# A mixture-of-experts layer on one core: when the weight splits of a step are made, how many buffers hold them, and in which order the last step does its work

## The chip, the cores and the metric

The kernel runs on one core of a Trainium2 chip. Times are device microseconds of one execution. The engines are TensorE (PE, with its weight loads as PEld), VectorE (DVE), ScalarE (ACT), GpSimd (POOL) and SyncE (SP, which here only issues DMAs). Each engine works through its own list of instructions in order and waits on semaphores.

## The reference

One layer (pooling mixer), then a mixture-of-experts MLP, then a final norm. The weights of the experts are 32 x (1024 x 1024 gate/up and 512 x 1024 down) float32, 201 MB in all, and are read once.

```
h = rms_norm(x, norm_mix); x = x + pool_mixer(h, pool_w, pool_scale)
h = rms_norm(x, norm_ffn)                       # 1024 tokens x 1024
g_sel = argmax(h @ w_rg + b_rg)                 # one of 4 groups
top 2 of the 8 experts of that group, gates = p_group * softmax share
for each expert e, its tokens:
    g, up = split(xt @ w_gu[e]); y = (silu(g) * up) @ w_down[e]
    x[tokens] += gate * y
return rms_norm(x, norm_final)
```

## The kernel before, in words

**Tiling.** The 32 experts are 32 steps; each gets one block of 128 rows (64 rows in the "small" steps 5, 7, ..., 27, which are handed the experts with few tokens). The rows are gathered from DRAM by POOL (`xg`), turned by PE (`turn_x`), and split into a high part (`x_hi`, ACT) and a low rest (`x_lo`, DVE), since fp32 products are made of three products of fp32r parts (hi x hi, hi x lo, lo x hi). The weights come as *pairs*: 1 MB each, 128 x 2048 float32, six to a step: four gate/up pairs and two down pairs, 192 in all, numbered in the order of use. `start(s) = 6 s - 2` is the number of the first gate/up pair of step s; pairs start(s)+4 and start(s)+5 are the down pairs of step s-1, used in step s.

**A pair's way.** SP loads it into a raw slot (L504; at most four loads in flight, L546; and a raw slot must be free, L540). ACT copies it to a high buffer (`split_pair`, L884). DVE subtracts (`low_pair`, L1210), and the low part takes the raw slot's place. PE uses both (12 matmuls for a full pair, L1724; 8 in a small step's gate/up pair, L1736) and frees both.

**Buffers.** There are 18 raw slots and 3 high buffers. `GIVEN` turns raw slots over to high buffers: two at step 4 (16 and 5) and two more at step 22 (14 and 7). Which slots are the last to be used, `end_raw`, follows from that; in the end five of them take the tiles of the output (`end_tile`) and the last step's h.

**A step on ACT** (`step` in the ACT program, from step 4 on). With n = `lead(s)`: split pairs up to start(s)+n; then, if step s-1 was small, `copy_lower`, `split_x_block(s)`, one more pair, `silu_of_sums(s-1)`; otherwise `silu_block(s-1)` and `split_x_block(s)`; pairs up to start(s)+n+2; `split_h_block(s-1)`; `copy_y` of step s-2, which POOL then scatters and adds to `total` in DRAM. `silu_block(s-1)` waits until PE has used the four gate/up pairs of step s-1. `lead` is 2, and 3 in step 29, 4 from step 30.

**A step on DVE** mirrors it with n = lead(s)-1: low parts up to start(s)+n; `add_lower`, `low_x`, one more low part and `hidden_of_sums` after a small step, otherwise `hidden` and `low_x`; low parts up to start(s)+n+3; `low_h`.

**A step on PE**: four gate/up pairs of s (with `turn_x(s+1)` ahead of the last), down pair, `turn_h(s)`, down pair. After a small step, `turn_h(s-1)` comes behind the first gate/up pair of s. Step 32 has only the two down pairs of step 31.

**The end.** When the scatter of step 28 has landed (`y_stored`), SP loads the eight tiles of `total` (L562) and POOL gathers the rows of the last three steps, whose y never goes through DRAM (L772). ACT makes eight sums of squares and roots (`final_square`, L816, L822) and three for the late rows (`late_squares`); DVE makes eight norms (`final_norm`, L1547, L1548), adds the last three y (`late_add_copied`, `late_add`) and makes three late norms. SP stores the eight tiles (L565); when all have landed, POOL scatters the late rows over them, one after the other (L777). ACT loads a table each time it goes between silu and square root.

Of the kernel before, what the change touches and what calls it, by code (L numbers as in the profile page):

```python
# [28 lines left out]
def hybrid_pool_moe(nc, x, norm_mix, norm_ffn, norm_final, pool_w, pool_scale,  # L29
# [3 lines left out]
    ALU, ACT, AX = mybir.AluOpType, mybir.ActivationFunctionType, mybir.AxisListType.X  # L33
# [3 lines left out]
    TILES = TOKENS // P  # L37
# [4 lines left out]
    E = w_re.shape[2]  # L42
# [9 lines left out]
    PER_STEP = (KD + KF) // 2  # L52
# [6 lines left out]
    HEAD = 4  # L59
    RANKED = E - HEAD - 3  # L60
    LATE, IN_BANKS = 3, 2
    FREE_STEP = HEAD
    GIVEN = {HEAD: 2, E - 10: 2}
    SPARE = sum(GIVEN.values())

    gu_rows = w_gu[0].rearrange("e (p k) f -> e p (k f)", k=KD)
# [8 lines left out]
    with ctx:  # L75
        def sem(name):
            return ctx.enter_context(nc.semaphore(name))
# [9 lines left out]
        def small(name, shape, dt):  # L87
            return ctx.enter_context(nc.sbuf_tensor(name, shape, dt))
# [34 lines left out]
        for m in range(MAIN):  # L123
            for _ in range(next((n for s, n in GIVEN.items() if m == s * PER_STEP - (PER_STEP - GU_PAIRS)), 0)):
                in_hi.append(in_raw.pop())
# [9 lines left out]
        end_free = [in_raw[r] + 1 for r in end_raw]  # L135
# [124 lines left out]
        eps = small("eps", [P, 1], f32)  # L260
# [4 lines left out]
        warm = small("warm", [P, 2], f32)  # L265
# [93 lines left out]
        pair_used = sem("pair_used")  # L359
# [15 lines left out]
        nfin_in = sem("nfin_in")  # L375
# [44 lines left out]
        def start(s):  # L420

            return s * PER_STEP - (PER_STEP - GU_PAIRS)

        def lead(s):

            return min(4, 2 + max(0, s - (E - LATE - 1)))

        def pw_low(eng, h):

# [29 lines left out]
        def place(m):  # L459

            s, j = next((s, j) for s in range(FREE_STEP, E + 1) for j in parts(s) if pair(s, j) == m)
            return s, s, j

        def up_to(following, one, s, n):

            while following[0] < min(start(s) + n, MAIN):
                one(*place(following[0]))
                following[0] += 1
# [341 lines left out]
        def _(act):  # L810
# [177 lines left out]
            def early_step(s):  # L988

                for j in parts(s):  # L990
                    if s == 0 and j == 0 or s == 1 and j < GU_PAIRS:
                        continue
                    if s > 1 and j == 0:
                        silu_block(s - 1, pair(s - 1, GU_PAIRS - 1) + 1)
                        split_x_block(s)
                    if s == 0 and j == 2:
                        router_exps()
                        act.wait_ge(slotted, 1)
                    if s == 0 and j == 3:
                        split_first_x()  # L1000
                    if s >= 1 and j == h_split_at(s):
                        split_h_block(s - 1, None if s == 1 else pair(s - 1, PER_STEP - 1) + 1)
                    split_pair(s, s, j)
                    if s >= 2 and j == h_split_at(s):
                        gates_of_y(s - 2)
                        copy_y(gate_now[:] if s == 2 else gate_all[:, s - 2:s - 1], start(s), None if s == 2 else s - 2)
                    if s == 0 and j == GU_PAIRS - 1:
                        split_x_block(1)
                        for m in range(2):
                            split_pair(1, 1, m)  # L1010
                        silu_block(0, GU_PAIRS, Y)
                        for m in (2, 3):
                            split_pair(1, 1, m)

            def step(s, s0, turn):
                if s < FREE_STEP:
                    early_step(s)
                    return
                n = lead(s)
                up_to(split_next, split_pair, s, n)  # L1020
                if s == E:

                    act.wait_ge(pair_used, end_free[TILES // 2])
                    for i in range(3):
                        final_square(i, 0)
                    nc.scalar.activation(warm[:, 1:2], eps[:], ACT.Silu)
                if is_small(s - 1):

                    copy_lower(s - 1, start(s - 1) + GU_PAIRS)
                    split_x_block(s)  # L1030
                    up_to(split_next, split_pair, s, n + 1)
                    silu_of_sums(s - 1, small_turn(s - 1, 0))
                else:
                    silu_block(s - 1, start(s - 1) + GU_PAIRS)
                    if s < E:
                        split_x_block(s, is_small(s))
                up_to(split_next, split_pair, s, n + 2)
                if s == E:
                    final_square(3, 0)
                    split_h_block(s - 1, end_free[TILES // 2], hi=h2_hi)  # L1040
                else:
                    split_h_block(s - 1, start(s))
                if s < E - 1:
                    copy_y(gate_all[:, s - 2:s - 1], start(s), s - 2)
                if s == E - 1:

                    up_to(split_next, split_pair, s, 2 * PER_STEP)
                    act.wait_ge(pair_used, start(s))
                    act.wait_ge(y_stored, 16 * (E - LATE))
                    col = E - LATE  # L1050
                    nc.scalar.activation(ysb[:], Y, ACT.Identity, scale=gate_all[:, col:col + 1])\
                        .then_inc(y_copied, 1)

            def final_square(i, turn):

                act.wait_ge(y_in[i], 16 * (turn + 1))
                root_mean_square(end_junk[:], end_tile(i), i, ss, rs).then_inc(squares3, 1)

            split_next = [FIRST]
# [5 lines left out]
            def late_squares(k):  # L1065

                act.wait_ge(late_sum, k + 1)
                root_mean_square(end_junk[:], late_tile(k), k, ss2, rs2).then_inc(late_square, 1)

            for i in range(4, TILES):  # L1070
                final_square(i, 0)
            for k in range(LATE):
                late_squares(k)

            with act.If(n):

# [29 lines left out]
        def _(dve):  # L1106
# [409 lines left out]
            def step(s, s0, turn):  # L1516
                if s < FREE_STEP:
                    early_step(s)
                    return
                n = lead(s) - 1  # L1520
                up_to(low_next, low_pair, s, n)
                if s == E:
                    up_to(low_next, low_pair, s, PER_STEP)
                    dve.wait_ge(nfin_in, 16)
                    for i in range(3):
                        final_norm(i, 0)
                if is_small(s - 1):
                    add_lower(small_turn(s - 1, 0))
                    low_x(s)
                    up_to(low_next, low_pair, s, n + 1)  # L1530
                    hidden_of_sums(s - 1)
                else:
                    hidden(s - 1)
                    if s < E:
                        low_x(s, is_small(s))
                up_to(low_next, low_pair, s, n + 3)
                if s == E:
                    late_add_copied()
                    final_norm(3, 0)
                    low_h(s - 1, hi=h2_hi, lo=h2_lo)  # L1540
                else:
                    low_h(s - 1)

            def final_norm(i, turn):

                dve.wait_ge(squares3, turn * TILES + i + 1)
                link(V.reciprocal(rs[:, i:i + 1], rs[:, i:i + 1]))  # L1547
                V.scalar_tensor_tensor(end_tile(i), end_tile(i), rs[:, i:i + 1], nfin[:],  # L1548
                                       ALU.mult, ALU.mult).then_inc(out_made, 1)

            def late_add_copied():

                dve.wait_ge(late_in[0], 16)
                dve.wait_ge(y_copied, E - IN_BANKS)
                V.tensor_tensor(late_tile(0), ysb[:], late_tile(0), ALU.add).then_inc(late_sum, 1)

            def late_add(k, y, dn_end):

                col = E - LATE + k
                dve.wait_ge(late_in[k], 16)  # L1560
                dve.wait_ge(pair_used, dn_end)
                V.scalar_tensor_tensor(late_tile(k), y, gate_all[:, col:col + 1], late_tile(k),
                                       ALU.mult, ALU.add).then_inc(late_sum, 1)

            low_next = [FIRST]
# [10 lines left out]
                V.scalar_tensor_tensor(late_tile(k), late_tile(k), rs2[:, k:k + 1], nfin[:],  # L1576
                                       ALU.mult, ALU.mult).then_inc(late_made, 1)

            for i in range(4, TILES):
                final_norm(i, 0)  # L1580
            late_add(1, Y, MAIN - GU_PAIRS // 2)
            late_add(2, GU, MAIN)
            for k in range(LATE):
                late_norm(k)
# [308 lines left out]
```

## Time and profile before

| | |
|---|---|
| time, median of 3 runs | 662.93 us (660.96 to 665.18) |
| profiled execution | 663.27 us, of which the span is 661.5 us |
| PE, DVE, ACT busy | 94%, 92%, 81% of the span |
| mean granted clock of TensorE | 0.983 |
| DMA traffic | 242.83 MB, mean 367 GB/s |

The span runs from the first to the last instruction; the rest of the execution's time lies around it. A busy share is an average over stages with different limits, so it tells less than the waits of each stage.

### The profile page before, as it was taken

What the parts mean: (1) busy time and instruction counts of PE and PEld (TensorE: products, weight loads), DVE (VectorE), ACT (ScalarE), POOL (GpSimd) and SP (SyncE); (2) the same over time, 40 slices, a digit from 0 to 9 for tenths busy, and PEclk for the clock granted to TensorE, in tenths of its full rate; (3) what the DMA queues carried; (4) which work ended last, traced back from release to release, by engine and by line L of the source; (5) the groups of instructions that cost most, each with busy time, mean ns of one, the idle gap of its engine ahead of it and who ended that gap; (6) DMA issues with size and microseconds to landing.
All of it is one profiled execution on the core that took longest, in us unless ns stands there. A gap on an engine that the chain in (4) does not pass through costs nothing.

```text
span 661.5 us, 9555 instructions
## 1 busy us (share of the span) xinstructions
PE 622.6 (94%) x3460; PEld 526.4 (80%) x3460; DVE 606.2 (92%) x501; ACT 535.7 (81%) x458; POOL 157.9 (24%) x127
## 2 busy tenths in 40 slices
PE   6899989999999999999999999897999989989983
PEld 4799978887888888888888888686877868767872
DVE  5887688989999999999999999897989889998987
ACT  5996626688898989898988988887879688978794
POOL 5000010032222222222222222252225222340311
PEclk9999989999999999999999999999999989989997
DMA  8997769999999999999999999999999999999985
GB/s 293 421 418 278 244 209 374 397 343 302 322 381 404 390 400 393 386 401 374 402 367 401 364 401 366 402 379 392 381 384 386 385 413 384 410 409 400 380 335 211
DMA packets 43637, 242.83 MB, mean 367 GB/s; under 512 B 8184, under 2 KB 9344, under 8 KB 19011
## 3 DMA queue, kind: packets, MB, share of 16 engines
q1 hardware_dynamic: 34322, 220.39, 84.2%
q0 software_dynamic: 9264, 21.79, 12.1%
q8 instruction: 29, 0.48, 0.3%
q14 instruction: 22, 0.17, 0.1%
HBM read 227.19 MB, written 26.21 MB: 383 GB/s over the span
## 4 chain that ended last, share of the span: by engine, by line
DMA 54%; PE 34%; DVE 5%; ACT 3%; issue 2%; SPq 0%; POOL 0%; ACTq 0%; POOLq 0%; DVEq 0%
DMA raw<-in_expert_w_gu 32%; PE psum L1724 19%; DMA raw<-in_expert_w_down 17%; PE psum L1736 3%; PE psum L1652 3%; PE psum L1670 2%; DMA total<-ysb,src_all 2%; PE psum L1638 2%; DMA raw<-total 1%; PE psum L1776 1%; DMA pw_in<-in_pool_w 1%; PE psum L1661 1%; DVE raw L1548 1%; PE psum L1678 1%; PE psum L1787 1%
## 5 line engine op out<-in xcount | busy, mean ns | idle before, releaser
L1210 DVE TENSOR_TENSOR w_lo<-raw,w_hi 128x2048 fp32r<-128x2048 f32 x113 | 255.4, 2284 | 7.8 <-ACT w_hi L884 7.4
L884 ACT ACTIVATE w_hi<-raw 128x2048 fp32r<-128x2048 f32 x113 | 213.5, 1914 | 21.8 <-DMA raw<-in_expert_w_gu 12.8
L1210 DVE TENSOR_TENSOR w_lo<-raw,w_lo 128x2048 fp32r<-128x2048 f32 x79 | 178.5, 2283 | 2.4 <-ACT w_lo L884 2.3
L884 ACT ACTIVATE w_lo<-raw 128x2048 fp32r<-128x2048 f32 x79 | 149.5, 1914 | 13.2 <-DMA raw<-in_expert_w_gu 10.2
L710 POOL DMA_INDIRECT total<-ysb,src_all x28 | 53.5, 1910 | 338.5 <-ACT ysb L979 323.9
L1724 PE MATMUL psum<-w_lo,x_hi 128*128 128x512 f32 x432 | 127.1, 397 | 5.8 <-DVE x_lo L1446 5.8
L1724 PE MATMUL psum<-w_lo,h_hi 128*128 128x512 f32 x376 | 108.3, 395 | 0.5 <-DVE h_lo L1480 0.5
L1724 PEld LDWEIGHTS psum<-w_lo,x_hi 128*128 128x128 f32 x432 | 81.0, 190 | 23.2 <-DVE x_lo L1446 6.7
L696 POOL DMA_INDIRECT xg<-normed,src_all x31 | 78.2, 2523 | 21.5 <-DVE src_all L1305 12.3
L1724 PEld LDWEIGHTS psum<-w_lo,h_hi 128*128 128x128 f32 x376 | 70.9, 190 | 15.5 <-DVE h_lo L1480 0.9
L1736 PE MATMUL psum<-w_lo,x_hi 128*128 128x512 f32 x276 | 74.0, 392 | 0.0
L1724 PE MATMUL psum<-w_hi,x_hi 128*128 128x512 f32 x208 | 67.2, 405 | 5.1 <-DVE x_lo L1446 5.1
L1724 PE MATMUL psum<-w_hi,x_lo 128*128 128x512 f32 x208 | 64.8, 393 | 0.0
L1736 PEld LDWEIGHTS psum<-w_lo,x_hi 128*128 128x128 f32 x276 | 51.5, 188 | 10.6
L1724 PEld LDWEIGHTS psum<-w_hi,x_hi 128*128 128x128 f32 x208 | 37.8, 191 | 13.6 <-DVE x_lo L1446 6.4
L970 ACT ACTIVATE h_hi<-psum 128x512 fp32r<-128x512 f32 x32 | 19.1, 597 | 34.9 <-PE psum L1787 20.0
L1724 PEld LDWEIGHTS psum<-w_hi,x_lo 128*128 128x128 f32 x208 | 39.3, 189 | 8.5
L1724 PE MATMUL psum<-w_hi,h_hi 128*128 128x512 f32 x136 | 42.9, 397 | 0.0
L1724 PE MATMUL psum<-w_hi,h_lo 128*128 128x512 f32 x136 | 42.0, 390 | 0.0
L1724 PE MATMUL psum<-w_lo,h_lo 128*128 128x512 f32 x120 | 37.5, 394 | 0.0
L1724 PE MATMUL psum<-w_lo,x_lo 128*128 128x512 f32 x112 | 35.5, 399 | 0.0
L1776 PEld LDWEIGHTS psum<-ident,xg 128*128 128x128 f32 x256 | 33.4, 191 | 2.5
(208 smaller groups left out, 865.4 us busy)
## 6 DMA issues: line engine op xcount, KB each, us to landing
raw<-in_expert_w_gu SPq DMA_DIRECT2D x128, 1024.0 KB, 10.9
raw<-in_expert_w_down SPq DMA_DIRECT2D x64, 1024.0 KB, 11.8
res<-in_x SPq DMA_DIRECT2D x8, 512.0 KB, 9.7
normed<-nx POOLq DMA_DIRECT2D x8, 512.0 KB, 7.3
total<-res SPq DMA_DIRECT2D x8, 512.0 KB, 8.7
raw<-total SPq DMA_DIRECT2D x8, 512.0 KB, 13.4
out<-raw SPq DMA_DIRECT2D x8, 512.0 KB, 3.9
pw_in<-in_pool_w SPq DMA_DIRECT2D x1, 1024.0 KB, 8.1
```

Of the source, the lines that this page charges most:

```text
L696: pool.indirect_dma_start(out=xg[0:slots, g, :], out_offset=None, in_=normed[:, :], in_offset=bass.IndirectOffsetOnAxis(ap=rows[0:slots].b ...
L710: pool.indirect_dma_start(out=total[:, :], out_offset=bass.IndirectOffsetOnAxis(ap=rows[0:slots].bitcast(u32), axis=0), in_=ysb[0:slots, : ...
L884: nc.scalar.activation(hi_at(s0, j), raw[q][:], ACT.Copy).then_inc(hi_done, 1)
L970: nc.scalar.activation(hi[:].rearrange("p k t -> p (k t)"), turned, ACT.Copy)\
L1210: V.tensor_tensor(w_lo[q][:], raw[q][:], hi_at(s0, j).bitcast(f32), ALU.subtract)\
L1548: V.scalar_tensor_tensor(end_tile(i), end_tile(i), rs[:, i:i + 1], nfin[:], ALU.mult, ALU.mult).then_inc(out_made, 1)
L1638: last = mm(PT[:, c0:c0 + width], x[:, par, cols], mask, start=(n == 0), stop=(n == len(terms) - 1))
L1652: last = mm(PY[:, g * 2 * P:(g + 1) * 2 * P], a[:, c, :], b[:, c, :], start=(n == 0), stop=(n == len(terms) - 1))
L1670: last = mm(sums, nxT[:, i % 2, c, :], wr[:, c, :], start=(c == 0), stop=(c == KD - 1))
L1724: last = mm(dst[:, n * N:(n + 1) * N], a[:, ch, :], b[:, c * D + n * N:c * D + (n + 1) * N], start=(ch == 0 and a is hi and b is b_hi), st ...
L1736: last = mm(dst[:, n * N:(n + 1) * N], parts_of[:, ch, :], b[:, c * D + n * N:c * D + (n + 1) * N], start=(ch == 0 and b is b_hi), stop=(c ...
L1776: last = nc.tensor.transpose(XT[:, c * P:(c + 1) * P], every(xg[:, g, :], KD, c), ident[:])
```

## The change

Three edits. `lead(s)` becomes 2 up to step 17 and 1 from step 18 on (before: 2, then 3 and 4 in the last steps); DVE's share, lead-1, becomes 0 from step 18. The two raw slots that were turned over at step 22 stay raw slots (16 raw, 5 high to the end), so that `end_raw` and `end_free` name other pairs. In the last step ACT does silu, the last splits and the high part of h ahead of all squares, and the order of squares is 0 to 5, late 0 and 1, 6, 7, late 2; DVE does `hidden`, the last low parts and `low_h` ahead of all norms, and then norms 0 to 4, the first two late adds, norms 5 to 7, the third late add, and the late norms. In step 31 ACT no longer makes the splits of pairs 190 and 191 ahead of its copy of y, which waits for `y_stored`.

```diff
-    GIVEN = {HEAD: 2, E - 10: 2}
+    GIVEN = {HEAD: 2}
+    LEAN = 18
...
         def lead(s):
-            return min(4, 2 + max(0, s - (E - LATE - 1)))
+            return 2 if s < LEAN else 1
...
                 up_to(split_next, split_pair, s, n)
-                if s == E:
-
-                    act.wait_ge(pair_used, end_free[TILES // 2])
-                    for i in range(3):
-                        final_square(i, 0)
-                    nc.scalar.activation(warm[:, 1:2], eps[:], ACT.Silu)
...
                 if s == E:
-                    final_square(3, 0)
                     split_h_block(s - 1, end_free[TILES // 2], hi=h2_hi)
...
                 if s == E - 1:
-                    up_to(split_next, split_pair, s, 2 * PER_STEP)
                     act.wait_ge(pair_used, start(s))
...
-            for i in range(4, TILES):
+            for i in range(6):
                 final_square(i, 0)
-            for k in range(LATE):
+            for k in range(2):
                 late_squares(k)
+            for i in range(6, TILES):
+                final_square(i, 0)
+            late_squares(2)
...
                 up_to(low_next, low_pair, s, n)
-                if s == E:
-                    up_to(low_next, low_pair, s, PER_STEP)
-                    dve.wait_ge(nfin_in, 16)
-                    for i in range(3):
-                        final_norm(i, 0)
...
                 if s == E:
-                    late_add_copied()
-                    final_norm(3, 0)
                     low_h(s - 1, hi=h2_hi, lo=h2_lo)
...
-            for i in range(4, TILES):
+            dve.wait_ge(nfin_in, 16)
+            for i in range(5):
                 final_norm(i, 0)
+            late_add_copied()
             late_add(1, Y, MAIN - GU_PAIRS // 2)
+            for i in range(5, TILES):
+                final_norm(i, 0)
             late_add(2, GU, MAIN)
```

## Rows read from the trace of the kernel before

**Rows 1.** Chain that ended last, from 590 us: start, us, what.

```profile
590.13 11.28 DMA raw<-in_expert_w_gu
...
610.70 12.05 DMA total<-ysb,src_all
622.77 9.67 DMA raw<-total
...
650.38 4.13 DMA out<-raw
```

**Rows 2.** Waits of SP, 500 to 600 us: total us, times, longest.

```profile
SPq L546 <- DMA raw<-in_expert_w_gu: 51.7, 23, 3.5
...
SPq L504 <- PE psum L1724: 0.2, 1, 0.2
```

**Rows 3.** Timeline, entry of step 28 (pair 166): start, us, instruction, [idle before].

```profile
558.26 1.92 ACT L884 ACTIVATE w_hi<-raw 128x2048 fp32r<-128x2048 f32 x1 [0.39 <-DMA raw<-in_expert_w_gu]
...
563.06 1.02 ACT L942 ACTIVATE lower<-psum 64x1024 f32<-64x1024 f32 x1
...
564.11 1.22 DVE L1462 TENSOR_TENSOR lower<-psum,lower 64x1024 f32<-64x1024 f32 x1 [1.31 <-ACT lower L942]
...
565.25 1.21 DVE L1446 TENSOR_TENSOR x_lo<-psum,x_hi 128x1024 fp32r<-128x1024 f32 x1
...
566.38 2.27 DVE L1210 TENSOR_TENSOR w_lo<-raw,w_lo 128x2048 fp32r<-128x2048 f32 x1
...
566.51 0.73 PE L1724 MATMUL psum<-w_hi,x_hi 128*128 128x512 f32 x2 [0.33 <-DVE x_lo L1446]
```

**Rows 4.** Timeline, step 29: split of pair 174, silu, turn of h.

```profile
581.22 1.91 ACT L884 ACTIVATE w_lo<-raw 128x2048 fp32r<-128x2048 f32 x1 [1.69 <-DMA raw<-in_expert_w_gu]
...
583.04 0.58 ACT L957 ACTIVATE silu<-psum 128x512 f32<-128x512 f32 x1
...
584.39 0.96 PE L1787 MATMUL psum<-ident,hid 128*128 128x128 f32 x4 [2.47 <-DVE hid L1476]
```

**Rows 5.** Windows: stretch, length, engines' busy us, PEclk, DMA share, GB/s.

```profile
423.00:426.00 3.00, 0.53 (x3) 0.10 (x1) 2.29 (x3) 2.98 (x3) 0.00 (x0) 1.00 1.03 432
426.00:429.00 3.00, 2.89 (x13) 2.26 (x13) 3.00 (x4) 2.86 (x3) 0.00 (x0) 1.00 1.03 418
...
584.40:588.00 3.60, 3.60 (x11) 3.02 (x12) 3.44 (x3) 3.15 (x3) 0.00 (x0) 0.55 1.02 418
```

**Rows 6.** Timeline of PE: first matmuls of pairs 170, 178, 182, 184, 188.

```profile
579.04 0.62 PE L1724 MATMUL psum<-w_hi,h_hi 128*128 128x512 f32 x2
...
607.96 0.62 PE L1724 MATMUL psum<-w_lo,x_hi 128*128 128x512 f32 x2
...
619.77 0.61 PE L1724 MATMUL psum<-w_lo,h_hi 128*128 128x512 f32 x2
...
625.72 0.62 PE L1724 MATMUL psum<-w_hi,x_hi 128*128 128x512 f32 x2
...
636.60 0.61 PE L1724 MATMUL psum<-w_lo,h_hi 128*128 128x512 f32 x2
```

**Rows 7.** Timeline of the last step: ACT and DVE.

```profile
633.69 1.28 ACT L822 ACT_TABLE_LOAD   x1
...
644.09 0.68 DVE L1480 TENSOR_TENSOR h_lo<-psum,h_hi 128x512 fp32r<-128x512 f32 x1
...
644.42 1.04 ACT L816 ACTIVATE end_junk<-raw 128x1024 bf16<-128x1024 f32 x1
...
645.78 1.04 ACT L816 ACTIVATE end_junk<-raw 128x1024 bf16<-128x1024 f32 x1
...
646.27 1.28 DVE L1548 SCALAR_TENSOR_TENSOR raw<-raw,rs,nfin 128x1024 f32<-128x1024 f32 x1
...
647.67 1.29 DVE L1548 SCALAR_TENSOR_TENSOR raw<-raw,rs,nfin 128x1024 f32<-128x1024 f32 x1
...
650.27 2.47 DVE L1562 SCALAR_TENSOR_TENSOR xg<-psum,gate_all,xg 128x1024 f32<-128x1024 f32 x2
```

## Prediction

> **What bounds the kernel now.** I read the chain that ended last first, because the busy shares (94%, 92%, 81%) single out no engine. Up to 601 us that chain is one load of weights behind the other; the last of them is the row at 590.13 [rows 1]. SP's own waits say the same: in 500 to 600 us it waited 51.7 us in 23 waits for the gate/up load four places ahead, and 0.2 us in one wait for a raw slot that PE had to free [rows 2]. So the DMA sets the pace of the middle, and the landing times of the pairs do not depend on what ACT, DVE and PE do as long as they keep up. What the other engines do decides only how far behind the landings PE runs, and that lag is paid once, at the end. The reader should see the lag in two places. PE begins pair 166 at 566.51, though it landed by 558.26 [rows 3]. And at 584.39 PE stood still 2.47 us for `hid` of step 28, because ACT first took in pair 174, for which it waited 1.69 us, and only then made silu [rows 4]. From there PE runs to the end with hardly a gap, a step in 17.76 us (607.96 to 625.72), and begins pair 188 at 636.60 [rows 6]. I call that moment G: all gate/up work of step 31 is done then, and silu of step 31 can start.
>
> The end itself hangs on a second thread: the scatter of step 28 (issued 610.70, 12.05 us), the loads of the output tiles behind it (issued 622.77, the first landed 9.67 us later), squares and norms, the last store (issued 650.38, landed 4.13 us later) and three late scatters behind its landing [rows 1]; the span ends at 661.5. From G to the last store's issue are 13.8 us, from that store's landing to the end 7.0 us.
>
> **The lead.** With lead 1, ACT makes x_hi and silu one landing earlier (three to four us in step 28), and in steps 29 to 31 two or three pairs earlier. I follow PE from pair 166. The pair lands at 558.26, ACT splits it to 560.2. Then comes `copy_lower`; in the trace PE began 3.45 us after that one's start (563.06 to 566.51) [rows 3], so x_lo would be done at 563.6. But with DVE's share at 0, low part 166 stands behind `add_lower` and `low_x`, where before it was made ahead of them. Its 2.27 us [rows 3] move onto the path: PE begins 166 at 566.0. Most of the earlier landing is thus given back, 0.5 us stays. After that PE has work without a stop, by its own distances in the trace [rows 3, 6]: to pair 170 12.53 us (578.5), to 172 as from 182 to 184, 5.95 (584.5), two steps of 17.76 (620.0), to 188 10.88: G = 630.9 in place of 636.6, 5.7 us earlier. The stall of 2.47 goes, since silu of step 28 then waits only for PE's pair 169; with it goes the slow stretch behind it, 3.6 us at a granted clock of 0.55, that is largely at 1.2 in place of 2.4 GHz, some 1.6 us lost [rows 5]; smaller stops are the rest.
>
> Are the inputs there in time? At a full step's entry DVE now has `hidden`, `low_x` and the low part in a row, 0.7 + 1.2 + 2.3 = 4.2 us plus 0.6 for silu, while PE has two down pairs and a turn, 5.95. That is enough by about 1 us, and by about 0.4 where DVE comes late out of the three low parts before (step 29). I take 0 for it and keep the bound for a rival.
>
> **The slots.** Two more raw slots touch only SP's wait for a free slot, 0.2 us in 100 [rows 2]: nothing. Five high buffers in place of seven make the split of pair p wait until PE has used p-5, four pairs (10.9 us) before PE needs it, against 1.9 + 2.3 us of work: nothing, at worst a few tenths in ACT's queue. `end_free` asks for pairs two earlier: nothing, since the loads wait for `y_stored`.
>
> **The wait that ACT now meets early.** In step 31 the copy of y waits for `y_stored` of step 28, and the splits of 187 to 190 now stand behind it. That scatter moves forward with PE: y of step 28 can be copied when pair 177 is used, which is 5.7 us earlier, so the scatter is issued near 605.0 and lands near 617.1 [rows 1, 6]. ACT reaches the wait at 620.0, when pair 183 is used. Then it copies (1.1), splits 187 (1.9), DVE makes the low part (2.3): 625.4, and PE wants it at 628.2. Cost nothing; it would start to cost if the scatter landed after 622.9. The output tiles are loaded 5 us earlier too, behind weights already queued, so they come somewhat earlier than 632.4 at best, and not later.
>
> **The last step.** Here is where it is paid back. Before, three squares and three norms ran in PE's shadow ahead of silu, and DVE's eighth norm ended at the last store's issue, G + 13.8. Now all eight come behind h. On DVE: silu starts at G + 0.15 and `hid` is done 1.35 later, as in [rows 4]; low parts 190 and 191 (2 x 2.27) to G + 6.05; `low_h` 0.68 to G + 6.7 [rows 3, 7]. On ACT: silu, split of 191 to G + 2.5; the high part of h waits for PE's pair 188 (2.7) and the turn, done at G + 4.0; the first square with its table load (1.28) and root is ready at G + 6.95; further ones follow every 1.36 (644.42 to 645.78). Norms go at 1.40 (646.27 to 647.67) [rows 7]. So norms 0 to 4 run from G + 7.05 to G + 14.05, two late adds of 1.24 (2.47 for two) to G + 16.5 [rows 7]. ACT, after square 5, must wait for the first late add (G + 15.3) with late square 0, then late square 1, and only then squares 6 and 7: ready at G + 19.6 and G + 21.0. DVE does norm 5 to G + 17.9, then stands until G + 19.8 and ends norm 7 at G + 22.6. With 4.13 + 7.0 the span ends at G + 33.7, where it was G + 24.9. The third late add and the late norms (1.24 + 3 x 1.40) are done at G + 28, before POOL asks for the last. PE's own last two down pairs start at G + 6.7 and end at G + 12.2: no longer near the end.
>
> A point on the tables first from the rows: the change takes out two of the three table loads of the last step, 1.28 us each [rows 7], 2.6 us of ACT. The Trainium skill ("ScalarE: Activation LUTs", Rules for kernel authors) says to group calls by table set and do all of one set before switching, and puts a switch at about 2.7 us with its drain; an estimate by that page is 5.3 us saved. The trace shows the 1.28 and no drain of such length (the root follows at once). By that rule the last step would get shorter; by my sum ACT's loads were not what the end waited for.
>
> **The sum.** 630.9 + 33.7 = 664.6 for the span, 3.1 more than 661.5: 5.7 gained before G, 8.8 lost behind it. The profiled execution took 1.8 more than its span, so 666.4 against its 663.3. The median of the runs, 662.93, lies 0.3 below that execution: I give 666.1. It would break even at G = 627.8.
>
> **The rivals.** What a measurement of this kernel can tell from no change is about 1%, 6.6 us.
>
> *The clock falls once more (0.2).* With PE further ahead, its stop before pair 166 grows from 0.33 us to between 1 and 2.7. After the 2.47 us stop the clock fell [rows 4, 5]; after the one before 426.11 (PE busy 0.53 us of three) it stayed at 1.00 [rows 5]. So it can go either way. Price 1.6 us: 667.7.
>
> *Faster (0.12).* The last step would be as long from G as before, 24.9, since ACT's and DVE's order there hides somewhere I don't see, and two table loads fewer take 2.6 off: 630.9 + 24.9 - 2.6 + 1.8 = 655.0 on the profiled execution, 654.7 on the median. For it: ACT's table loads did stand between silu and squares. Against it: DVE has 19 us of norms and adds that by their place in the list cannot start before `low_h`.
>
> *Slower by over 1% (0.16).* DVE falls behind at the entries of full steps. With 16.2 us of work (six low parts of 2.27, 1.2 for x, 0.7 each for `hid` and h) in each 17.76 us step it has little to give; if the low part behind `low_x` comes late by more than the 0.4 to 1 us of room, each of the entries 29, 30 and 31 can lose up to a whole low part, 2.27: G + 6.8, 672.9. It decides once `low_x` ends later than 2.3 us before PE's need. For it: 92% busy. Against it: by my count it just fits.
>
> *The edits do not reach the time (0.07).* PE stays where it was, because the landings or the small steps hold it, and the early squares were worth little: 661 to 665.
>
> **The numbers.** Forecast 0.45, the others as given: faster by over 1% (below 656.3) 0.12; slower by over 1% (above 669.6) 0.16; within 0.72. Most of the cases within 1% lie in 661 to 669.5; to leave out no more than two in ten the range goes from 658.5, half way to the faster case, to 670.0, just into the slower one.
>
> **What would show it.** Right: pair 166 begins near 566 with its low part last; no stop of PE at the turn of h in step 29; pair 188 about 5.7 us earlier against the landings; a single table load in the last step; the last store's issue some 22 us behind pair 188 and a wait of ACT for the first late add. Wrong: pair 188 later than 634 (DVE or the clock), ACT waiting for the scatter in step 31, or the first norm starting before `low_h`.

## The result, and the profile after

The changed kernel takes 666.80 us in the median of 20 runs against 663.03 of the kernel before (20 runs too); the ratio is 1.0056, 95% interval 1.0042 to 1.0069. Two of the 20 runs of the kernel before took 886 and 1249 us and are not in the ratio; its other 18 lie between 661.0 and 666.0. That is slower by an amount clear of noise, and within the 1% that the chances call the same. Forecast were a time of 666.1 us (0.7 below the median measured) and a span of 664.6; the profiled execution has a span of 664.7 (time 666.56). That the span was met to 0.1 us is partly luck: two errors cancelled, as told below.

I count by pairs: "L166" is the landing of pair 166 (the first of step 28), "P188" PE's first matmul of pair 188, when all gate/up work of step 31 is done and silu of step 31 can start. The forecast's G is P188.

| | L166 | L166 to P188 | P188 to end | span |
|---|---|---|---|---|
| before | 558.3 | 78.3 | 24.9 | 661.5 |
| forecast | 558.3 | 72.6 | 33.7 | 664.6 |
| after | 560.0 | 72.5 | 32.3 | 664.7 |

(Each entry is rounded by itself.)

The entry of step 28 in the timeline of the kernel after (start, us, engine, line, instruction, idle time before it), to be held against [rows 3]:

```profile
560.00 1.92 ACT L885 ACTIVATE w_hi<-raw 128x2048 fp32r<-128x2048 f32 x1 [1.70 <-DMA raw<-in_expert_w_gu]
...
561.94 1.02 ACT L943 ACTIVATE lower<-psum 64x1024 f32<-64x1024 f32 x1
...
564.14 1.20 DVE L1442 TENSOR_TENSOR x_lo<-psum,x_hi 128x1024 fp32r<-128x1024 f32 x1
565.27 2.27 DVE L1206 TENSOR_TENSOR w_lo<-raw,w_hi 128x2048 fp32r<-128x2048 f32 x1
...
567.69 0.70 PE L1717 MATMUL psum<-w_hi,x_hi 128*128 128x512 f32 x2 [3.45 <-DVE w_lo L1206]
```

The reader sees what ended PE's wait: in [rows 3] it was `x_lo`, now it is the low part of the pair, which stands behind `x_lo` on DVE. From the landing to the first matmul are 7.7 us; the forecast had 566.0 - 558.3 = 7.7. In step 29 the turn of h, at which PE stood still for 2.47 us in [rows 4], has no wait:

```profile
582.82 0.64 PE L1780 MATMUL psum<-ident,hid 128*128 128x128 f32 x4
...
632.45 1.07 PE L1717 MATMUL psum<-w_lo,h_hi 128*128 128x512 f32 x4
```

The second row is P188. The last step on ACT and DVE, against [rows 7]: silu comes before all squares, one table load is left, norm 0 starts at P188 + 7.0, and ACT waits 1.49 us for the first late add ahead of late square 0, so that squares 6 and 7 come late and DVE stands 1.69 us ahead of norm 6.

```profile
632.65 0.60 ACT L958 ACTIVATE silu<-psum 128x512 f32<-128x512 f32 x1 [2.01 <-PE psum L1717]
...
637.77 1.28 ACT L823 ACT_TABLE_LOAD   x1
...
638.28 0.69 DVE L1476 TENSOR_TENSOR h_lo<-psum,h_hi 128x512 fp32r<-128x512 f32 x1
...
639.46 0.16 DVE L1536 RECIPROCAL rs<-rs 128x1 f32<-128x1 f32 x1 [0.49 <-ACT rs L823]
...
647.69 1.06 ACT L817 ACTIVATE end_junk<-xg 128x1024 bf16<-128x1024 f32 x1 [1.49 <-DVE xg L1544]
...
651.93 0.16 DVE L1536 RECIPROCAL rs<-rs 128x1 f32<-128x1 f32 x1 [1.69 <-ACT rs L823]
```

The end of the chain that ended last, of the kernel after (start, us, what), where before stood [rows 1]:

```profile
650.53 1.05 ACT end_junk L817 x2
651.61 0.30 ACT rs L823
652.13 1.28 DVE raw L1537
653.52 1.30 DVE raw L1537
654.84 2.63 DMA out<-raw
657.52 0.79 issue
658.32 0.54 POOL out L778
```

### The profile page after: what moved, and what is told of

Read it like the earlier page. It is cut to its first block, busy times and chain, and to the rows that moved or that the text cites. A ratio compares the mean times of both kernels' runs of the same rounds, so it can differ in the third digit from the quotient of the medians.

```text
span 664.7 us, 9551 instructions
## 1 busy us (share of the span) xinstructions
PE 623.0 (94%) x3460; PEld 527.2 (79%) x3460; DVE 605.9 (91%) x501; ACT 531.3 (80%) x455; POOL 138.0 (21%) x127
## 4 chain that ended last, share of the span: by engine, by line
DMA 52%; PE 36%; DVE 6%; ACT 3%; issue 2%; SPq 1%; POOL 0%; ACTq 0%; POOLq 0%; DVEq 0%
DMA raw<-in_expert_w_gu 35%; PE psum L1717 23%; DMA raw<-in_expert_w_down 16%; PE psum L1645 3%; PE psum L1663 2%; PE psum L1631 2%; PE psum L1769 1%; DVE raw L1537 1%; PE psum L1729 1%; DMA pw_in<-in_pool_w 1%; PE psum L1654 1%; PE psum L1671 1%; DVE w_lo L1206 1%; PE psum L1780 1%; ACT end_junk L817 1%
## 5 line engine op out<-in xcount | busy, mean ns | idle before, releaser
L1206 DVE TENSOR_TENSOR w_lo<-raw,w_hi 128x2048 fp32r<-128x2048 f32 x124 | 279.6, 2285 | 10.5 <-ACT w_hi L885 10.1
L885 ACT ACTIVATE w_hi<-raw 128x2048 fp32r<-128x2048 f32 x124 | 233.1, 1913 | 14.0 <-PE psum L1717 7.2
L1206 DVE TENSOR_TENSOR w_lo<-raw,w_lo 128x2048 fp32r<-128x2048 f32 x68 | 153.6, 2285 | 3.4 <-ACT w_lo L885 3.3
L885 ACT ACTIVATE w_lo<-raw 128x2048 fp32r<-128x2048 f32 x68 | 128.1, 1912 | 3.0 <-DMA raw<-in_expert_w_gu 2.3
L1717 PE MATMUL psum<-w_lo,h_hi 128*128 128x512 f32 x352 | 101.7, 393 | 0.0
L1717 PE MATMUL psum<-w_hi,x_hi 128*128 128x512 f32 x220 | 70.5, 402 | 8.0 <-DVE w_lo L1206 8.0
L1729 PE MATMUL psum<-w_lo,x_hi 128*128 128x512 f32 x268 | 72.6, 392 | 0.0
L697 POOL DMA_INDIRECT xg<-normed,src_all x31 | 62.3, 2011 | 21.5 <-DVE src_all L1301 12.4
L1717 PE MATMUL psum<-w_hi,h_hi 128*128 128x512 f32 x160 | 50.9, 399 | 0.5 <-DVE h_lo L1476 0.5
L1717 PE MATMUL psum<-w_hi,h_lo 128*128 128x512 f32 x160 | 49.5, 391 | 0.0
L1729 PE MATMUL psum<-w_hi,x_hi 128*128 128x512 f32 x116 | 36.4, 395 | 0.0
L1717 PEld LDWEIGHTS psum<-w_hi,h_lo 128*128 128x128 f32 x160 | 30.0, 188 | 6.4
```

Of the source, the lines that this page charges most:

```text
L697: pool.indirect_dma_start(out=xg[0:slots, g, :], out_offset=None, in_=normed[:, :], in_offset=bass.IndirectOffsetOnAxis(ap=rows[0:slots].b ...
L885: nc.scalar.activation(hi_at(s0, j), raw[q][:], ACT.Copy).then_inc(hi_done, 1)
L1206: V.tensor_tensor(w_lo[q][:], raw[q][:], hi_at(s0, j).bitcast(f32), ALU.subtract)\
L1717: last = mm(dst[:, n * N:(n + 1) * N], a[:, ch, :], b[:, c * D + n * N:c * D + (n + 1) * N], start=(ch == 0 and a is hi and b is b_hi), st ...
L1729: last = mm(dst[:, n * N:(n + 1) * N], parts_of[:, ch, :], b[:, c * D + n * N:c * D + (n + 1) * N], start=(ch == 0 and b is b_hi), stop=(c ...
```

## The experiments

The table has all eleven runs. Each gives a ratio to the kernel before, and from its profiled execution the two stretches. L166 is left out: it differs from run to run between 557.8 and 560.4, so two spans can differ by up to 2.6 us for that alone, while the stretches compare more closely. A profiled execution is also only one of several: its time lies up to 2.0 us from the median of its kernel's runs (slots only: 673.62 against 675.66), so a ratio and a span need not agree.

| run | ratio (95%) | L166 to P188 | P188 to end | span |
|---|---|---|---|---|
| lead only | 1.0024 (1.0007 to 1.0041) | 74.7 | 30.5 | 664.8 |
| last step only | 1.0107 (1.0077 to 1.0136) | 78.0 | 32.3 | 669.4 |
| slots only | 1.0190 (1.0159 to 1.0222) | 85.2 | 28.8 | 671.9 |
| before, lead 2 to the end | 1.0016 (1.0000 to 1.0032) | 75.2 | 30.4 | 664.2 |
| after, seven high buffers | 1.0047 (1.0029 to 1.0065) | 72.5 | 32.3 | 663.9 |
| after, low part ahead | 1.0037 (1.0023 to 1.0050) | 73.1 | 32.3 | 664.3 |
| after, squares in order | 1.0011 (0.9994 to 1.0029) | 72.5 | 30.5 | 661.4 |
| after, these with early late add | 1.0009 (0.9992 to 1.0026) | 73.0 | 30.3 | 663.7 |
| after, end in order | 1.0011 (0.9995 to 1.0026) | 73.7 | 29.4 | 661.5 |
| the same, low part ahead after small steps | 1.0006 (0.9990 to 1.0023) | 71.4 | 29.4 | 660.2 |
| lead 2 to the end and slots | 1.0040 (1.0026 to 1.0053) | 74.6 | 30.1 | 662.4 |

### The lead alone

```diff
     GIVEN = {HEAD: 2, E - 10: 2}
+    LEAN = 18
...
-            return min(4, 2 + max(0, s - (E - LATE - 1)))
+            return 2 if s < LEAN else 1
```

> Only the lead is changed (2, then 1 from step 18; DVE's share 0); slots and last step as before. My theory: PE reaches pair 188 some 5.8 us sooner after the landing of pair 166 (72.5 us in the changed kernel, 78.3 before), but with the squares ahead of silu the gain cannot reach the end: the first square waits for the first output tile, which the saturated DMA lands between 632 and 635 us whatever PE does, and from there to the end are 29 us as before. Span 661.5 to 663.5 against 661.5, ratio 1.000 to 1.003. Rival (the lead is a plain gain that the last step then loses): span near 656, ratio 0.992.

Measured: 1.0024; P188 at 634.29, 3.6 us sooner after L166 than before, and the end 30.5 us after it. The gain before P188 does not reach the end; the rival's 0.992 is excluded. Timeline of this run, last step:

```profile
634.69 1.06 ACT L817 ACTIVATE end_junk<-raw 128x1024 bf16<-128x1024 f32 x1 [0.49 <-DMA raw<-total]
...
640.20 1.28 ACT L1027 ACT_TABLE_LOAD   x1
...
641.60 0.58 ACT L958 ACTIVATE silu<-psum 128x512 f32<-128x512 f32 x1
...
642.95 1.13 PE L1788 MATMUL psum<-ident,hid 128*128 128x128 f32 x4 [5.68 <-DVE hid L1477]
```

ACT waits for the first output tile, then does three squares and a table load before it comes to silu, and PE stands still for 5.68 us. The silu starts at 641.60 though PE was ready for it at 634.3. So with an earlier PE the old order of the last step is the wrong one, and the tile's landing (634.6) leads from there on. It lands 2.2 us later than in the kernel before (632.44, [rows 1]), though it was asked for 1.3 us earlier; 1.4 us of that is only that all landings of this run are later (L166 is 559.6). I had expected 72.5 us to P188; of the 2.2 missing, 1.6 are a slow clock that this run had in step 28 (last section), and 0.5 is a stop just ahead of pair 188, whose cause is told under "Lead 2 to the end".

### The last step alone

```diff
     GIVEN = {HEAD: 2, E - 10: 2}
-            return 2 if s < LEAN else 1
+            return min(4, 2 + max(0, s - (E - LATE - 1)))
```

(as a change of the kernel after, whose last step is kept)

> Only the last step is changed (silu and h ahead of squares and norms, the new order of squares and norms, the splits of 190 and 191 behind the copy of y); lead and slots as before. My theory: from pair 188 to the end are 32.2 to 33.7 us in place of 24.9, with pair 188 where it was, 636.6: span 668.8 to 670.3, ratio 1.011 to 1.013. Rival (two table loads fewer are worth their time): span 659, ratio 0.996.

Measured: 1.0107 (just under the 1.011 expected), span 669.4, and 32.3 us from P188 (637.18) to the end, to the tenth as in the kernel after. The new order of the last step costs 7.4 us by itself when PE is not earlier. The rival on table loads is excluded: two loads fewer are there, and the stretch is longer.

### The slots alone

```diff
-    GIVEN = {HEAD: 2, E - 10: 2}
+    GIVEN = {HEAD: 2}
```

> Only the two raw slots of step 22 stay raw slots (16 raw, 5 high). My theory: nothing, ratio 0.998 to 1.002, since SP waited 0.2 us in 100 for a slot and a high buffer is free four pairs ahead; with lead 3 and 4 in steps 29 to 31 ACT may now meet a full set of high buffers, at worst some tenths of a microsecond. Rival (high buffers matter at that lead): ACT waits for PE ahead of silu in steps 29 to 31 and the span grows by 2 us or more, ratio 1.003 or more.

Measured: 1.0190. My theory was wrong and the rival right, by far more than it asked. Timeline of this run, steps 29 and 30:

```profile
602.29 1.91 ACT L884 ACTIVATE w_hi<-raw 128x2048 fp32r<-128x2048 f32 x1 [0.80 <-PE psum L1724]
604.11 0.58 ACT L957 ACTIVATE silu<-psum 128x512 f32<-128x512 f32 x1
...
605.46 0.75 PE L1787 MATMUL psum<-ident,hid 128*128 128x128 f32 x4 [3.27 <-DVE hid L1476]
...
610.66 1.92 ACT L884 ACTIVATE w_lo<-raw 128x2048 fp32r<-128x2048 f32 x1 [5.06 <-PE psum L1724]
```

With lead 4, ACT must split pairs up to start(s)+3 ahead of silu of step s-1, and with five high buffers the last of these may start only when PE has used pair start(s)-2, the down pair behind the gate/up pairs for which silu waits. So silu comes one down pair too late, and PE stops at each turn of h (in steps 29, 30 and 31 for 1.8, 3.3 and 3.3 us). ACT's wait of 5.06 us for PE in the last row shows that each engine then waits for the other. A high buffer is not "free four pairs ahead" if the order of ACT's list makes the split stand ahead of silu.

### Lead 2 to the end

```diff
-            return min(4, 2 + max(0, s - (E - LATE - 1)))
+            return 2
```

> The kernel before with lead 2 to the end, that is without its 3 and 4 in the last steps, and nothing else. My theory: most of the earlier pair 188 comes from the ramp, not from lead 1: the 2.5 us stop in step 29, the slow clock behind it (1.6) and the 0.6 in step 30 go, so from the landing of pair 166 to pair 188 are 73 to 74 us in place of 78.3. The end does not follow, for the same reason as with the lead alone: span 661 to 663, ratio 0.999 to 1.003. Rival (lead 1 is what moves PE): 77 us or more for that stretch.

Measured: 1.0016; 75.2 us to P188, of which 1.0 us is a stop just ahead of pair 188; without it 74.2, just above the theory's 73 to 74. Taking the 3 and 4 out of the last steps gives most of the earlier P188 (3.1 to 4.1 of 5.8 us). The end does not follow; PE stops for 5.8 us at the last turn of h, as with the lead alone.

The stop ahead of pair 188 has its cause in a part of the change that neither the forecast nor this expectation priced. Timeline of this run:

```profile
630.76 1.92 ACT L884 ACTIVATE w_hi<-raw 128x2048 fp32r<-128x2048 f32 x1 [1.42 <-DMA raw<-in_expert_w_down]
...
632.59 1.09 ACT L1051 ACTIVATE ysb<-psum,gate_all 128x1024 f32<-128x1024 f32 x1
...
633.78 1.17 PE L1724 MATMUL psum<-w_lo,h_hi 128*128 128x512 f32 x4 [1.00 <-issue]
```

The trace names no releaser, but PE's program waits for ACT's copy of y before the down products, and that copy ends at 633.68. In the old order it stands behind the splits of pairs 190 and 191, so here it waits for their landings. In the four runs that have this order and an early PE or a late copy (lead only, slots only, this one, and lead 2 with the slots) pair 188 starts 0.10 to 0.11 us behind the end of the copy, after stops of 0.5, 0.4, 1.0 and 1.2 us. In the kernel before the copy ended at 631.62, 5 us ahead of pair 188; in the kernel after it ends at 623.4.

### Lead 2 and the slots together

```diff
-    GIVEN = {HEAD: 2, E - 10: 2}
+    GIVEN = {HEAD: 2}
...
-            return min(4, 2 + max(0, s - (E - LATE - 1)))
+            return 2
```

> The kernel before with both: lead 2 to the end and the two raw slots kept raw (16 raw, 5 high). My theory: five high buffers hurt only under lead 3 and 4, so this is as the kernel with lead 2 and seven: ratio to before 1.000 to 1.003, and no wait of ACT for PE ahead of silu of more than 1 us in steps 29 to 31. Rival (five hurt at lead 2 as well): 1.006 or more.

Measured: 1.0040, just over the theory's 1.003 and well under the slots' 1.019; 74.6 us to P188 (1.2 of them the stop behind the copy of y), and ahead of silu no wait for PE but one of 0.69 us for a high buffer. So the 1.9% are the product of two edits, five high buffers under a lead of 4. Whether five cost some 0.2% at lead 2 stays open: the interval overlaps that of seven (1.0000 to 1.0032), and the profiled execution shows no place for it.

### After, with seven high buffers

```diff
-    GIVEN = {HEAD: 2}
+    GIVEN = {HEAD: 2, E - 10: 2}
```

> The changed kernel with the two raw slots turned over at step 22 again (14 raw, 7 high). The slots alone made the old lead 1.9% slower, since ACT, taking in pairs up to four ahead before silu, ran out of high buffers. My theory: at lead 1 ACT never needs more than five, so seven are worth nothing: as the changed kernel, ratio to before 1.004 to 1.007, 72 to 73 us from the landing of pair 166 to pair 188. Rival (five high buffers hold the changed kernel back too): 1 to 3 us shorter from pair 166 to 188, ratio 1.003 or less.

Measured: 1.0047, both stretches as in the kernel after (72.5 and 32.3). At lead 1 the slots are worth nothing, as forecast.

### After, with the low part ahead

```diff
-                n = lead(s) - 1
+                n = 1
...
-                up_to(low_next, low_pair, s, n + 3)
+                up_to(low_next, low_pair, s, n + 3 if s < LEAN else n + 2)
```

> The changed kernel, but DVE makes the low part of a step's first pair ahead of add_lower and low_x again (its bounds 1, 2, 3 in place of 0, 1, 3), and in the last step that of pair 190 ahead of hidden. My theory: the low part (2.3 us) leaves the path of the entry of step 28, 1 us comes back at the second pair, and the last step's norms start 1 us sooner: from the landing of pair 166 to its first matmul 5.4 to 5.7 us in place of 7.7, pair 188 1 to 2 us earlier, span 1 to 2.5 us shorter than the changed kernel, ratio to before 1.001 to 1.004. Rival (the entry is held by x_lo and the turn of h alike): the first matmul earlier, pair 188 not.

Measured: 1.0037; the first matmul of pair 166 comes 6.8 us after the landing in place of 7.7, and P188 no earlier (73.1); the last step is as long as in the kernel after (32.3). The rival was right. The ratio falls into the theory's range all the same, but its interval (1.0023 to 1.0050) overlaps that of the kernel after (1.0042 to 1.0069). Timeline of this run, entry of step 29:

```profile
578.41 0.60 ACT L958 ACTIVATE silu<-psum 128x512 f32<-128x512 f32 x1 [0.32 <-PE psum L1717]
...
579.33 2.29 DVE L1206 TENSOR_TENSOR w_lo<-raw,w_lo 128x2048 fp32r<-128x2048 f32 x1
...
581.53 0.68 DVE L1472 TENSOR_TENSOR hid<-silu,psum 128x512 f32<-128x512 f32 x1
...
582.26 0.75 PE L1780 MATMUL psum<-ident,hid 128*128 128x128 f32 x4 [1.17 <-DVE hid L1472]
```

At a full step the low part now stands ahead of `hidden`, and PE stops for 1.17 us at the turn of h. So the low part has a right place on each kind of step: ahead of `low_x` after a small one, behind `hidden` after a full one.

### After, with the squares in order

```diff
-            for i in range(6):
+            for i in range(TILES):
                 final_square(i, 0)
-            for k in range(2):
+            for k in range(LATE):
                 late_squares(k)
-            for i in range(6, TILES):
-                final_square(i, 0)
-            late_squares(2)
```

> The changed kernel with ACT's squares in the order 0 to 7, then late 0 to 2; DVE as it is. My theory: the 1.5 us for which ACT waits for the first late add, and the two late squares that stand ahead of squares 6 and 7, cost the eighth norm 1.9 us: it ends at pair 188 + 20.5 in place of 22.4, and the span is 1.5 to 2 us shorter, ratio to before 1.002 to 1.004. Rival (DVE is full there anyway, or the last store and the late scatters set the end): no difference from the changed kernel.

Measured: 1.0011, P188 to the end 30.5 us in place of 32.3, norm 7 at P188 + 20.6 in place of 22.4. The theory holds: the order of ACT's squares alone costs 1.8 us of the last step. Between the two ratios (1.0056 and 1.0011) lie 3.0 us; the intervals allow 1.8, and what the rest is stays open.

### All of these, with the first late add moved up

```diff
+                if s == E:
+                    up_to(low_next, low_pair, s, 0)
+                    late_add_copied()
                 up_to(low_next, low_pair, s, n)
...
-            for i in range(5):
+            for i in range(TILES):
                 final_norm(i, 0)
-            late_add_copied()
             late_add(1, Y, MAIN - GU_PAIRS // 2)
-            for i in range(5, TILES):
-                final_norm(i, 0)
```

(with the edits of the two runs above)

> The changed kernel with DVE's low part ahead, squares and norms 0 to 7 in order ahead of the late ones, and the first late add moved into DVE's free time ahead of the low part of pair 190. My theory: pair 188 at 630.5 to 631.5, norm 0 begins near 637.5, norm 7 ends 11.2 us later, the three late norms are done by the time POOL may scatter: span 659 to 661, so 4 to 5.5 us shorter than the changed kernel and 0 to 2 us shorter than before, ratio 0.996 to 1.000. Rival (the output tiles, of which the saturated DMA lands the last at 643, hold the end): 662 or more, since norm 7 would wait for its tile.

Measured: 1.0009, span 663.7: 2.7 us above the range, of which 2.1 are a later L166 (560.4). Late add and low part together, ahead of `hidden`, made PE stop 0.62 us at the last turn of h and brought the high part of h to P188 + 4.3 (637.74), 0.9 later than in the kernel after; square 0 stands behind it on ACT, and so norm 0 began at P188 + 7.9 in place of 7.0. The rival's reason was wrong too: the tiles had landed before their squares (the first at 635.5, its square began at 638.5).

### After, with the end in order

```diff
                 up_to(low_next, low_pair, s, n)
+                if s == E:
+                    late_add_copied()
...
-            for i in range(5):
+            for i in range(TILES):
                 final_norm(i, 0)
-            late_add_copied()
             late_add(1, Y, MAIN - GU_PAIRS // 2)
-            for i in range(5, TILES):
-                final_norm(i, 0)
```

(with the squares in order; the low parts as in the kernel after)

> The changed kernel with squares 0 to 7 ahead of the late ones on ACT, and on DVE the first late add in the free 0.9 us ahead of hidden of the last step, norms 0 to 7 without a break behind h, then the other late adds; lead and low parts as in the changed kernel. My theory: norm 0 begins at pair 188 + 7.0 as before, norm 7 ends at pair 188 + 18.2 to 18.5 (22.4 in the changed kernel, 20.6 with the squares alone in order), and the late scatters go as soon as the last store has landed: from pair 188 to the end 29.3 us, span 660 to 661.5, ratio to before 0.998 to 1.001. Rival (the early late add delays h, as it did with the low part ahead): 30 us or more.

Measured: 1.0011, 29.4 us from P188 to the end, as expected. L166 to P188 was 73.7, since ACT began the split of pair 166 only 1.1 us after its landing. I put that down to a stop of PE of 3.7 us in step 26 with a slow clock behind it (532 to 536 us), which no run tests. The chain's end in this run: eight norms without a break, the last store, and POOL.

```profile
647.71 1.28 DVE raw L1536
649.10 1.30 DVE raw L1536
650.42 3.92 DMA out<-raw
654.39 0.79 issue
```

### The same, with the low part ahead after small steps only

```diff
-                n = lead(s) - 1
+                n = 1 if s < LEAN or is_small(s - 1) else 0
...
-                up_to(low_next, low_pair, s, n + 3)
+                up_to(low_next, low_pair, s, 4 if s < LEAN else 3)
```

> As the kernel with the end in order, and in addition DVE makes the low part of a step's first pair ahead of add_lower and low_x, but only in steps that follow a small one, not at the full steps 29 to 32. My theory: from the landing of pair 166 to its first matmul 6.8 us in place of 7.7 and to pair 169 0.8 us less; no stop at the turn of h in step 29, so pair 188 comes 71.6 to 71.8 us after that landing (72.5 in the changed kernel) and the span is 0.8 us shorter than its partner. Rival (a stop of 1.2 us at the turn of h takes it back, as with the low part ahead everywhere): 72.5 us or more.

Measured: 1.0006 (0.9990 to 1.0023); 71.4 us to P188, the shortest of all runs, 29.4 to the end, span 660.2, the lowest. Against the kernel after it wins back its 0.5%; from the kernel before it can't be told apart. Against its partner, the kernel with the end in order, the medians show nothing (663.26 and 663.33 us). By the stretches PE is 6.9 us earlier at P188 than in the kernel before and the last step 4.5 us longer, because its norms start only behind h; the 2.4 us that this leaves do not show in the medians.

## Why the prediction was right

**The middle is the DMA's.** Confirmed: SP's waits for slots are 0.2 us in 500 to 600 us after as before, and the landings differ little whatever ACT, DVE and PE do. L166 itself was 1.7 us later in the profiled execution of the changed kernel. Of that 0.8 was there when ACT split pair 60 (262.14 us against 261.35), where both kernels still do the same. The rest may be chance or the lead: the eight profiled executions with lead 1 have L166 between 558.4 and 560.4 (mean 559.3), the five with the old lead or lead 2 between 557.8 and 559.2 (mean 558.3). Whether lead 1 itself makes the landings later stays open.

**The lead.** L166 to P188 was forecast 72.6 and is 72.5, and 72.5 again in two of its variants. Its parts held: the low part moved onto the path (7.7 us from the landing), the stop in step 29 gone, nothing lost at the entries of full steps. Of the 5.7 us the forecast put 0.5 down to the entry of step 28, where lead 2 becomes 1, and the rest to the stops from step 29 on, where the lead was 3 and 4. The entry is worth 0.6 to 1.5. In all five profiled executions with lead 2 there, pair 166 starts 5.4 us after ACT begins to split pair 167, which is 2.9 us after L166 in two of them and 3.6 to 3.8 in the others, so 8.3 to 9.2 us after L166; with lead 1 and the low part last it no longer waits for pair 167 and starts 7.7 us after L166 (four executions; a fifth, with the end in order, is late for its own reason). I had taken the 0.5 from an execution with the short distance. Behind pair 166 the stretch to P188 was 70.1 us before, 65.0 with lead 2 to the end without the stop ahead of pair 188, and 64.8 in the kernel after: the rest of the gain is indeed the 3 and 4 taken away (with the copy of y moved ahead, so that no stop takes back 1.0 of it), and lead 1 is worth next to nothing there.

**The clock.** The forecast left it open. The stop ahead of pair 166 grew to 3.45 us, more than the 1 to 2.7 I gave, and the clock held all the same; in the runs with the lead alone and with the last step alone it fell there.

**The slots.** Forecast "nothing, at worst a few tenths", and in this change they are nothing. But the reason was incomplete. The seven high buffers were what the old lead 4 lived on; the two edits belong together, and taken alone the slots cost 1.9%. "Free four pairs ahead" left out what stands behind the split in ACT's list.

**ACT's wait for the scatter in step 31.** Forecast without cost, and right: ACT copied y at 622.3, straight after the high part of h, which had waited for PE; the scatter had landed at 617.4. What the forecast left out is a gain. Had the copy stayed behind the splits of 190 and 191, PE would have met it: it ended at 631.6 before, and the forecast wanted pair 188 at 630.9. The runs with the old order show that stop (0.5 to 1.2 us with lead 1 or 2).

**The output tiles.** Here a step failed: "The output tiles are loaded 5 us earlier too", and "they come somewhat earlier than 632.4 at best, and not later". In the kernel after the first landed at 634.4, in the run with the lead alone at 634.6. The chain that ended last in the run with the lead alone has this load:

```profile
621.46 13.15 DMA raw<-total
```

The scatter had landed at 618.4 in that run (617.4 in the kernel after), but SP still had the last weights to issue, as its four loads in flight allow, and came to the first tile only at 621.5 (621.0). So the tile was asked for 1.7 us earlier than before in the kernel after, not 5, and took 13.4 us in place of 9.7. Before, the three late gathers were issued behind the first tile; now two of them stand ahead of it (618.3 and 619.6), and all share the same DMA engines with the last weights. That this order makes the difference is read from the issues and was not tried. Measured from L166 the tile lands 74.2 us later before, 74.4 in the kernel after and 75.0 with the lead alone: the earlier request brings nothing. It cost the changed kernel nothing, since square 0 began only at 636.60.

**The last step.** The mechanism was right, the size 1.4 us too large: 32.3 against 33.7. Norm 7 ended at P188 + 22.4 (forecast 22.6); the last store landed in 2.63 us, where I took 4.13 from a row of before (what makes this differ is open, see the last section). That and the later L166 (1.7) cancelled by luck, so the total is closer than its parts.

**The rivals.** The faster one asked that the last step stay as long as before and that two table loads fewer take 2.6 us off. It did not: with three loads there are 24.9 us from P188 (before) and 30.5 (lead alone), with one 32.3 (last step alone, and after). The Trainium skill's rule ("ScalarE: Activation LUTs", Rules for kernel authors) to group calls by table set is followed by the changed kernel, and the trace shows 1.28 us for a load and no drain beside it (the square before it ended at 637.76, the load runs from 637.77, the root starts at 639.07). The load that is left is on the chain that ended last; but the same edit put the squares and norms behind h, and that cost more than two loads. What the two loads are worth by themselves no run shows. The slower one, DVE late at full steps, did not come: PE had no stop at the entries of steps 29 to 31.

## What to carry to other kernels

When an engine is made earlier, ask at once what stands in the queues behind it: here 5.8 us on PE were gained before the last step and lost again either to squares that waited for a tile ahead of silu, or to norms that waited for h. Ask also what an earlier engine will now meet: the copy of y, 5 us early before, would have stopped PE. A count of buffers and a count of pairs taken in ahead are one setting, not two: here five buffers in place of seven cost 1.9% under a lead of 4, 0.2% or nothing under a lead of 2, and nothing under a lead of 1. What an engine takes in ahead of an instruction that a consumer waits for must not need a buffer which that consumer frees later. And the place of an instruction in an in-order list should differ with the kind of step it is in, if the steps differ in what PE can do meanwhile.

## What the runs showed of the hardware

The same kind of stop ahead of the same pair leaves the clock alone in one execution and not in another. Windows of the kernel after (stretch, its length, busy us of PE, PEld, DVE, ACT, POOL, granted clock, DMA share, GB/s), and then of the run with the lead alone:

```profile
564.20:567.70 3.50, 0.05 (x2) 0.04 (x1) 3.50 (x4) 3.50 (x3) 0.00 (x0) 1.00 1.02 424
567.70:571.00 3.30, 3.30 (x17) 2.83 (x18) 3.30 (x3) 0.43 (x1) 0.00 (x0) 1.00 1.03 429
```

```profile
564.10:567.30 3.20, 0.00 (x0) 0.01 (x1) 3.20 (x3) 3.20 (x3) 0.00 (x0) 0.97 1.02 430
567.30:570.60 3.30, 3.28 (x8) 2.62 (x9) 3.30 (x3) 0.46 (x1) 0.00 (x0) 0.51 1.01 427
```

After 3.45 us without work PE ran on at 1.00, that is 2.4 GHz; after 3.25 us it ran at 0.51, nearly all at 1.2 GHz, and did 8 matmuls where it did 17. Of the other stops ahead of pair 166, one of 3.31 us (last step only) was followed by 0.58, and those of 2.64 (slots only), 3.07 (lead 2 to the end), 3.22 (seven high buffers) and 3.50 us (squares in order) by 1.00. The longer stops at the last turn of h, 5.68 to 6.15 us in three runs, were each followed by 0.50. What decides between the short ones stays open; the 1.6 us that such a stop may cost can't be priced from a single profile.

Stores of 512 KB output tiles, issued 1.4 us apart, landed in 2.6 to 2.7 us in one stretch and in 3.3 to 3.9 in another. The first are the last three of the run with the squares in order, ahead of which no store had been issued for 3.7 us (in the kernel after the last three, behind pauses of 3.7 and 3.2 us); the second are those of the run with the end in order, where eight followed each other without a pause. But the pause alone is not the cause. The first store of the run with the last step alone was issued 2.5 us after the last tile had landed, with no DMA traffic in between, and took 3.88 us. And with the lead alone the five stores behind a pause of 4.2 us took 2.61, 2.64, 2.70, 2.99 and 4.13. The cause stays open.
